# A hybrid attention and convolution layer: high-and-low-part projections of 256 columns, head norms on three engines, and convolution and top-k work moved to ScalarE

## The reference, cut to what matters

```python
h = rmsnorm(x);  proj = h @ w_in            # q, k, v (512 each), idx_q, idx_k, idx_w, glu, gate_a, gate_c
q, k = rmsnorm over each head of 64 (8 heads)
score = sum_h idx_w[h] * relu(idx_q[h] . idx_k)      # top_k = 256 keys of each query
attn = softmax over the selected keys (q.k/8 + relative bias) @ v
u = glu_a * sigmoid(glu_b);  c = depthwise_conv(u, 31 taps), 512 channels;  c = silu(layernorm(c))
merged = sigmoid(gate_a) * (attn @ w_attn_out) + sigmoid(gate_c) * (c @ w_conv_out)
x = x + merged @ w_out;  x = x + swiglu(rmsnorm(x))
```

## Time and profile before

| | before |
|---|---|
| runs, median of 3 | 2069.97 us (2067.32 to 2075.99) |
| the profiled execution, its own time | 2071.23 us |
| its span in the trace | 2069.3 us |
| busy in the span: PE, DVE, ACT, POOL | 94%, 55%, 31%, 18% |
| chain that ended last | PE 83%, POOL 5%, DVE 4%, issue 4%, ACT 3% |
| PE's idle time in the qkv stage, 523 to 698 us | 28 of 175 us |

### The profile page before, as it was taken

The page is one execution under the profiler, slowest core; times in us unless marked ns, Lnnn a source line. Parts: engine busy times, 40 slices in busy tenths (PEclk is TensorE's granted clock), DMA queues, the critical chain, the costliest instruction groups (busy, mean ns, idle before and its releaser), DMA issues.

```text
span 2069.3 us, 26437 instructions
## 1 busy us (share of the span) xinstructions
PE 1935.9 (94%) x10080; PEld 1549.9 (75%) x10080; DVE 1138.4 (55%) x1700; ACT 637.5 (31%) x1161; POOL 377.6 (18%) x331
## 2 busy tenths in 40 slices
PE   6968999999888986898999989999999999999998
PEld 3533899999433433566994459999999999999997
DVE  1054899999999946776442233333343333433333
ACT  2244322221233126676101122322233222322232
POOL 1101122664477802341000000000000000000000
PEclk9998999999999997999999999999999999999999
DMA  6340112321331253673522223333343333433332
GB/s 204 89 75 20 62 42 76 95 97 57 138 132 61 82 173 96 217 258 149 190 99 92 81 81 111 130 124 122 122 153 122 122 125 131 163 129 122 122 122 101
DMA packets 86606, 242.37 MB, mean 117 GB/s; under 512 B 14549, under 2 KB 32373, under 8 KB 77315
## 3 DMA queue, kind: packets, MB, share of 16 engines
q1 hardware_dynamic: 81643, 227.34, 32.4%
q10 hardware_dynamic: 4896, 14.16, 1.7%
HBM read 211.68 MB, written 26.61 MB: 115 GB/s over the span
## 4 chain that ended last, share of the span: by engine, by line
PE 83%; POOL 5%; DVE 4%; issue 4%; ACT 3%; SPq 1%; DMA 1%; POOLq 0%; DVEq 0%; ACTq 0%
PE ps L642 20%; PE ps L640 20%; PE ps L641 20%; PE ps L966 6%; PE ps L670 4%; PE ps L788 4%; DVE buf L1390 2%; POOL buf L1774 2%; PE ps L863 1%; PE ps L840 1%; POOL buf L1782 1%; PE ps L882 1%; PE ps L823 1%; PE ps L722 1%; PE ps L853 1%
## 5 line engine op out<-in xcount | busy, mean ns | idle before, releaser
L640 PE MATMUL ps<-buf,buf 128*128 128x384 f32 (+2 forms) x2220 | 771.6, 348 | 8.8 <-DVE buf L1339 7.5
L642 PE MATMUL ps<-buf,buf 128*128 128x384 f32 (+2 forms) x2220 | 773.9, 349 | 0.0
L641 PE MATMUL ps<-buf,buf 128*128 128x384 f32 (+2 forms) x2220 | 772.5, 348 | 0.0
L640 PEld LDWEIGHTS ps<-buf,buf 128*128 128x128 f32 x2220 | 418.2, 188 | 28.3 <-DVE buf L1339 5.7
L641 PEld LDWEIGHTS ps<-buf,buf 128*128 128x128 f32 x2220 | 418.5, 188 | 17.9
L642 PEld LDWEIGHTS ps<-buf,buf 128*128 128x128 f32 x2220 | 418.0, 188 | 18.0
L1339 DVE TENSOR_TENSOR buf<-buf,buf 128x1024 fp32r<-128x1024 f32 (+4 forms) x216 | 301.3, 1397 | 176.4 <-ACT buf L1317 39.0
L1641 DVE TENSOR_TENSOR buf<-buf,ps 128x384 f32<-128x384 f32 x66 | 36.6, 555 | 401.6 <-PE ps L642 401.6
L1403 DVE TENSOR_SCALAR_CACHE_REDUCE buf<-buf,buf 128x384 uint8<-128x384 f32 (+6 forms) x231 | 218.3, 1009 | 1.2
L1446 DVE SCALAR_TENSOR_TENSOR buf<-buf,buf,buf 128x1024 f32<-128x1024 f32 x210 | 200.6, 996 | 3.7
L788 PE MATMUL ps<-buf,buf 128*128 128x512 f32 x432 | 193.5, 605 | 4.2 <-DMA buf<-hT_scr 4.2
(11 more groups left out here) (169 smaller groups left out, 1659.3 us busy)
## 6 DMA issues: line engine op xcount, KB each, us to landing
buf<-in_w_ffn SPq DMA_DIRECT2D x67, 1024.0 KB, 5.7
buf<-in_w_ffn SPq DMA_DIRECT2D x66, 512.0 KB, 3.6
buf<-in_cache_k SPq DMA_DIRECT2D x16, 1024.0 KB, 7.5
buf<-in_cache_v SPq DMA_DIRECT2D x16, 1024.0 KB, 10.2
buf<-hT_scr SPq DMA_DIRECT2D x27, 512.0 KB, 3.4
buf<-in_w_cols SPq DMA_DIRECT2D x24, 512.0 KB, 4.4
buf<-in_x SPq DMA_DIRECT2D x18, 512.0 KB, 5.0
gate_scr<-buf ACTq DMA_DIRECT2D x16, 576.0 KB, 5.4
```

What stands on the lines that cost most here:

```text
L640: mm(dst, whi, xhi, start=start, stop=False)
L641: mm(dst, whi, xlo, start=False, stop=False)
L642: return mm(dst, wlo, xhi, start=False, stop=stop)
```

## The change

- **Products.** k, q and v are projected as 6 pieces of 256 columns (k, k, q, q, v, v), 9 token tiles each: 54 tiles `q` of 24 fp32r products of 256 columns (high x high, high x low, low x high). The high and low parts of h, which the column stage made, stay in SBUF and are used from there; h is no longer written to `hT_scr` nor loaded back. The weights' high part is made on ACT (`qkv_high`), the low one on DVE (`qkv_low`).
- **Norms** of the 36 k and q tiles: ACT squares the whole tile, DVE sums each head (`head_sums`), POOL makes the inverse root of 4 heads (`inverse_norm`), DVE scales straight from PSUM (`scale_heads`), POOL applies the gain (`gain`). PE transposes tile q-3 behind tile q, and tile q waits until tile q-4 has been scaled.
- **Search.** The two largest score tiles (1024 and 1152 keys) are counted on ACT, by the sum of signs of threshold minus score (`sign_step`), in 7 of every 9 groups of the column stage and ahead of the evacuation of that group. DVE waits in each step for both. Behind the 32 steps, DVE repairs the threshold of these two tiles (four passes over a tile) and counts once more.
- **Convolution.** POOL adds 23 taps of channel tile 3: 5 of its own, and 18 whose products ACT makes in the column stage from tile 14 on (`tap_product`, `tap_sum`). DVE does 101: 38 after the masks and before its first `head_sums`, 23 spread between the 36 tiles, 40 after them.
- The layouts of h, of the attention's probabilities and of several buffers change, loops on ACT, POOL and SP are written out, and the mask goes to HBM when column tile 22 has been asked for.

```diff
-        POOL_TAPS = CK // 2
+        OWN_TAPS, POOL_TAPS, TAP_TILE = 5, 23, NGLU + 6
@@ SyncE
-            for t in range(NT):
-                sp.wait_ge(S("hT_made"), 2 * t + 2)
-                sp.dma_start(A["hT_scr"][t].rearrange("p (k t) -> p k t", k=KD), hT[:, :, tok(t)])\
-                    .then_inc(S("hT_out"), 16)
...
+            for t in range(12, NCOL):
+                sp.wait_ge(S("col_done"), NG * (t - 3))
+                col_in(t // 4, t % 4)
+                if t == NCOL - 2:
+                    sp.wait_ge(S("mask_made"), NSEL)
+                    sp.dma_start(A["mask_scr"], scoreS).then_inc(S("mask_out"), 16)
@@ TensorE
+            def project(q):
+                f, t = divmod(q, NT)
+                if t == 0:
+                    pe.wait_ge(S("qkv_split"), f + 1)
+                if q < NQK:
+                    if q >= 4:
+                        pe.wait_ge(S("scaled"), q - 3)
...
+                for k in range(KD):
+                    mm(qkv_bank(q), hhi[:, t, k], wqhi[f][:, k], start=k == 0, stop=False)
+                    mm(qkv_bank(q), hhi[:, t, k], wqlo[f][:, k], start=False, stop=False)
+                    l = mm(qkv_bank(q), hlo[:, t, k], wqhi[f][:, k], start=False, stop=k == KD - 1)
+                l.then_inc(S("qkv_done"), 1)
+
+            for q in range(NQ):
+                project(q)
+                if 3 <= q < NQK + 3:
+                    turn(q - 3)
@@ ScalarE
+            def sign_step(g):
+                step = g - 2 * (g // 9) - (g % 9 > 4)
+                if g % 9 in (4, 8) or step >= 32:
+                    return
+                act.wait_ge(S("thr_made"), step + 1)
...
+                for c in range(NG):
+                    sign_step(t * NG + c)
                     act.wait_ge(S("col_done"), t * NG + c + 1)
...
+                    n = 2 * (t - TAP_TILE) + c - 1
+                    if c and 0 <= n < POOL_TAPS - OWN_TAPS:
+                        tap_product(n)
...
+                if t == NCOL - 5:
+                    qkv_high(0)
@@ VectorE
             for bit in range(31, -1, -1):
-                count(ALU.is_ge)
...
+                count(ALU.is_ge, tiles[own])
+                value = -1.0 if bit == 31 else float(1 << bit)
+                ch.add(ve.tensor_scalar(flip[:, own], cnt[:, own], float(TOPK), value, ALU.is_lt, ALU.mult))
+                dve.wait_ge(S("signs_made"), NSIGN * (32 - bit))
+                ch.link(ve.tensor_tensor(diff, cnt[:, other], kvec, ALU.subtract))
+                ch.link(ve.tensor_scalar(flip[:, other], diff, 0.0, value, ALU.is_gt, ALU.mult))
...
-            dve.wait_ge(S("out_state"), 48)
-            ve.memset(biasS, 0.0).then_inc(S("biasS_zero"), 1)
+            dve.wait_ge(S("mask_out"), 16)
...
+            TAPS_BEFORE, TAPS_BETWEEN = 38, 23
+            qkv_low(0)
+            for j, d in all_taps[:TAPS_BEFORE]:
+                conv_tap(j, d)
...
+            between = all_taps[TAPS_BEFORE:TAPS_BEFORE + TAPS_BETWEEN]
+            for q in range(NQK + 1):
+                if q < NQK:
+                    head_sums(q)
+                    if q % NT == 5:
+                        qkv_low(q // NT + 1)
+                    elif q > 1 and q % 4 != 1:
+                        conv_tap(*between.pop(0))
+                if q:
+                    scale_heads(q - 1)
...
+            dve.wait_ge(S("turn_made"), NQK)
+            ve.memset(biasS, 0.0).then_inc(S("biasS_zero"), 1)
+            for j, d in all_taps[TAPS_BEFORE + TAPS_BETWEEN:]:
+                conv_tap(j, d)
@@ GpSimd
+            for q in range(NQK + 1):
+                if q < NQK:
+                    inverse_norm(q)
+                if q:
+                    gain(q - 1)
```

More of the change, by code:

```diff
@@ L76 @@
 SLOTS = 6
+HW = AW // 2
+NQK, NQ = 4 * NT, 6 * NT
 def bucket_rows():
@@ L1182, in layer_norm @@
+            act.wait_ge(S("mask_made"), NSEL)
+            for q in range(NQK + 3):
+                if q < NQK:
+                    squares(q)
+                if q >= 3:
+                    turned(q - 3)
+                if q % NT == 3:
+                    qkv_high(q // NT + 1)
+            qkv_high(5)
+            for t in range(NT):
+                values(t)
             def layer_norm(k, c):
@@ L1402, in count @@
+            def count(op, tiles):
+                for j, (n, (sc, L)) in enumerate(tiles):
+                    if j >= 2:
                         ch.wait(1)
-                    ch.add(ve.tensor_scalar(hits[n % 2][:, 0:L], sc, thrf[:, n:n + 1], None, op, ALU.add,
+                    ch.add(ve.tensor_scalar(hits[j % 2][:, 0:L], sc, thrf[:, n:n + 1], None, op, ALU.add,
                                             accum_out=cnt[:, n:n + 1]))
                 ch.wait()
+            tiles = list(enumerate(select))
@@ L1419, in _ @@
+            ch.link(ve.tensor_scalar(diff, diff, 1.0, 3e38, ALU.subtract, ALU.mult))
+            ch.link(ve.tensor_tensor(least, least, diff, ALU.add))
+            ch.link(ve.tensor_tensor(thrf[:, other], thrf[:, other], least, ALU.max))
+            count(ALU.is_gt, tiles[other])
             ch.link(ve.tensor_scalar(rest, cnt, -1.0, float(TOPK), ALU.mult, ALU.add))
@@ L1459, in _ @@
+            assert not between
+            qkv_low(5)
+            dve.wait_ge(S("qn_made"), NQK)
+            dve.wait_ge(S("turn_made"), NQK)
+            ve.memset(biasS, 0.0).then_inc(S("biasS_zero"), 1)
+            for j, d in all_taps[TAPS_BEFORE + TAPS_BETWEEN:]:
                 conv_tap(j, d)
@@ L1784, in _ @@
-            for c in range(2):
-                qk_norm(c, 0, True)
-                with pool.Fori(1, NG) as i:
-                    ch.loop(i - 1, 12)
-                    qk_norm(c, i, False)
-                ch.done(NG - 1)
-            while taps < POOL_TAPS:
-                conv_tap(CT - 1, taps)
-                taps += 1
+                if t > NGLU and own < OWN_TAPS:
+                    own_tap(own)
+                    own += 1
+                if t >= TAP_TILE:
+                    for _ in range(2):
+                        tap_sum(added)
+                        added += 1
```

427 lines of the change are left out of this document (219 added, 208 removed).

## The result

The changed kernel takes 2087.87 us (median of 4 runs, 2086.28 to 2088.55) where the kernel before takes 2072.09 us beside it (2067.32 to 2075.99). The ratio is 1.0076, with a 95% interval of 1.0052 to 1.01: slower, by about 16 us. The forecast was 2067 us and no change. The range (2052 to 2090) holds the time, but no change was forecast and the kernel got slower; the rival that names the same time, late signs, turns out not to be how it came about.

The account below looks back on a forecast made before the run. PE and POOL were taken to set the attention's start, DVE 15 us behind. Taps from 484.5, tile 4 to 563, loop to 675, last taps to 752 instead of 754.6: 2071.2 - 2.7 = 2068.5, against the median 2067 us; range 2052 to 2090.

Parts of the forecast that it names:

- late signs: Rival, search: ACT's signs come late, a step takes 6.2 us, all behind slips 22 us: 2089 us; chance 0.14.
- part 2: Search and its cover: 5.5 us a step, steps end at 415 us, masks at 477, DVE's taps begin at 484.5.
- masks 43.5: 477 us: Masks on DVE behind the search: 43.5 us as before, ending at 477 us, 46 us earlier than before.
- part 1: PE's projection products: 256 columns at 0.117 us each, 3.1 us a tile for k and q, 2.8 for v.
- weight-load rival: Rival, PE's projection: a weight load bounds 256-column products at 0.188 us, 51 us more: 2118 us; chance 0.07.
- 16 us for held-back signs: Search: in three glu tiles ACT waits 5.3 us for POOL's product and holds back a sign, 16 us.
- part 3: Taps ahead of the norms: 38 taps and a copy take 70.5 us, to 555; tile 4 ends at 563.
- the 14 taps of the earlier trace: Taps in the profile before, taken as without POOL: 25.4 us, 1.82 each, used to price DVE's taps.
- part 4: Loop of 34 more tiles with norms: 3.3 us a tile, between PE's 3.1 and 3.9 with all stalls, ending at 675 us.
- part 5: Last 40 taps behind the last transposed tile: 76.5 us, to 752 us; DVE bounds the attention's start.
- Mutual exclusion of DVE and POOL: Rival, projection loop: POOL's 2.2 us and a tap's 1.8 add up, 3.7 us a tile in the mean: 2080 us; chance 0.07.
- 62-us stretch: Evidence against exclusion, from the profile before: some 32 taps worth 59 us ran beside seven POOL tiles worth 33 us.

Follow-up runs that it names:

- 2052-us kernel: Changed kernel with POOL's 18 helped taps on DVE, last channel tile first, first weight's low part after 12 taps, 45 taps in the loop: 2052.25 us, ratio 0.9893.

## Why the prediction was wrong

The step that failed is in part 2: "masks 43.5: 477 us". It took the masks' duration from rows of before and moved it, without asking what ran on POOL in the new place. Step by step against the trace:

1. **PE's products (part 1): right.** Consecutive products of 256 columns start at 637.90, 638.01, 638.13, 638.25 us, 0.117 apart:

```profile
637.78 0.28 PE L815 MATMUL ps<-buf,buf 128*128 128x256 f32 x1
...
638.25 0.28 PE L816 MATMUL ps<-buf,buf 128*128 128x256 f32 x1
```

The weight-load rival (0.188) falls.

2. **The search (part 2): the right end by wrong terms.** 415 us was forecast, and the first of the last seven counts starts at 416.1. But a free step is 4.80 us, not 5.0, the mean is 6.0, not 5.5, and the 16 us for held-back signs did not come: ScalarE did idle 16.0 us for GpSimd's product, yet DVE waited for a sign once, 1.1 us. What lengthens steps is POOL, stop by stop: 22 small operations that overlap it are 37 us longer together, of the 39 us by which the 32 steps exceed 32 free ones. The rival of late signs, which gave 2089 us, fits the measured time and not the trace.
3. **Final counts and repair: 23 us, not 18**; here too plain small instructions met sums (16 us without them).
4. **The masks: 67.5 us, not 43.5.** Before, a part of 44 us already was such stops, 7.7 us of them over a free 36.0. In the new place there are 14 POOL instructions and not 7, at 2.3 us each. The sums are POOL work that the change itself put there: two a tile, from column tile 14 on, exactly when the shorter search brings the masks forward. The 3.4 us for the masks' transfer are missing in the forecast as well. Taps began at 512.6 us and not at 484.5: 28 us late.
5. **Taps ahead of the loop (part 3): 76.4 us, not 70.5.** A low part and six sums of POOL held seven instructions of the first four taps, 16.5 us together; a tap beside the sums took 6.3 us. The others took 1.58 and not 1.82: the stretch of the 14 taps of the earlier trace rows was not without POOL, which worked beside its first 8 us and lengthened it by 3.3 us.
6. **The loop (part 4): the length right, the cause wrong.** From the first sum of a head to the clearing of `biasS` it took 118.8 us; the forecast has 120. It ran at 105.2/35 = 3.0 us a tile, which is TensorE's pace, with 3.1 forecast for that and 3.3 for POOL. POOL pays for the collisions here: its gain of 256 columns takes 0.73 to 1.73 us, but has time for it.

```profile
L1882 POOL TENSOR_TENSOR buf<-buf,buf x36: 727/740/1730, 592.1 to 697.5; 128x256 f32<-128x256 f32 x36
```

7. **The last 40 taps (part 5): 65.5 us, not 76.5**, again the 1.58. That DVE and not TensorE would bound the attention's start was right.

The sum closes: 752 + 28 (late taps) + 6 - 1 - 11 = 774 us, with 773.3 measured.

Mutual exclusion of DVE and POOL was priced in one place alone, the loop, with a chance of 0.07. There it falls: 3.0 us a tile, not 3.7. In the masks the traces show it nearly in full, 2.0 to 2.3 us for each 2.4 to 2.7-us instruction of POOL. The 62-us stretch that was held against it is real evidence, but of other work. The 1.82 us for a tap that went into it held stops; yet with every instruction at its shortest in that trace, 50.7 us of DVE's work and 33.2 us of POOL's still lie in those 62 us. What overlapped was above all POOL's root of 8 columns (L1774), 1.64 us long. From the profile before, POOL's root and a tap's instruction beside it, then POOL's gain of 512 columns and the 128-column half of a tap, which is 0.34 us long when free:

```profile
547.20 1.64 POOL L1774 TENSOR_TENSOR buf<-buf 128x8 f32<-128x8 f32 x1
547.36 1.28 DVE L1446 SCALAR_TENSOR_TENSOR buf<-buf,buf,buf 128x1024 f32<-128x1024 f32 x1
...
550.04 2.13 POOL L1782 TENSOR_TENSOR buf<-buf,buf 128x512 f32<-128x512 f32 x1
550.97 1.35 DVE L1446 SCALAR_TENSOR_TENSOR buf<-buf,buf,buf 128x128 f32<-128x128 f32 x1
```

The root holds nothing, the wide gain does; beside all 18 roots of that trace, DVE's taps lose 0.3 us together. So the stretch with narrow roots said nothing about masks beside wide low parts and sums. The Trainium skill ("SBUF — State Buffer", Who interferes with whom) has the lock, held for a whole instruction by whichever engine issued first. The masks agree with it; the roots do not, as a tap with two SBUF inputs that starts 0.16 us behind a root runs at its free 1.28 us, and here the measurement decides. The mistake was to ask the question about the loop and not about the place where the plain instructions of the masks would land.

So where did a large change's gain go? The signs and the shorter steps bring the masks forward by 40 us. The masks give back 24 of these, and the held instructions of the first four taps 16.5. On top comes VectorE's new work in the loop: it takes over sums, scalings and low parts from POOL and ACT there and fills 76.5 of 114 us, 38 of them idle at TensorE's pace, while 38 taps wait in front of the loop and 40 behind it. The experiments give back both parts: 39 us by leaving out the sums, 9 us (by the attention's start) by 7 more taps in the loop, and 36 us by the 2052-us kernel, with every tap done.

## What to carry to other kernels

When work is moved in time, look at who else is awake in its new place, and reprice every instruction of it there: a duration is a property of the slot as much as of the instruction. Count the helper engine's wide instructions beside VectorE's plain ones; where each stops it for nearly its whole length, as here, giving the helper a task of 2.7 us to save one of 1.58 is a loss. And when a stretch of the trace is used as evidence on a collision, check that the same forms of instructions meet in it. Once one engine bounds a stretch, its idle time inside loops that another engine paces is the place to put its leftover work.

## What the hardware showed that I had not expected

Whether VectorE is stopped by GpSimd depends on the form of its instruction: counts (a comparison that sums up as it goes) ran beside GpSimd's `tensor_tensor` at their free durations in every trace here, while an operation on 128 by 5 numbers took 2.3 us in place of 0.17. Work of GpSimd is therefore free beside the search's counts, and dear beside the small operations at a step's end, the masks and the taps. The sums over heads (L1515, `tensor_reduce`) kept their 0.42 us beside POOL too, and so did the scalings (L1523, one input from PSUM). POOL's form counts as well: its roots of 8 columns held no tap. No experiment here changed the form of a DVE instruction to see its stops come or go. The same section of the Trainium skill names both cases: it excepts the `tensor_scalar` that also writes out its accumulator, and `tensor_reduce`, from the lock, and the traces agree.

A tap of 1024 and 128 columns takes 1.58 us on VectorE when GpSimd is silent, and 6.3 beside its sums, 2.7 to 3.7 for each of its two instructions, while the sums themselves take 3.2 us each in place of 2.7 (two in 5.49 us beside counts): the two take turns.
